# The low-rank gate's rows placed beside the queries' columns in the opening of a two-block transformer kernel

## The reference, cut to what matters

```
h = rms_norm(x, norm_mix_g[l]) * (1.0 + sc_m) + sh_m
proj = jnp.einsum('bsd,de->bse', h, w_in[l])
(a_q, a_k, a_v, b_q, b_ff, b_fb, b_i, b_g,
 c_q, c_k, c_v, c_g, c_lrf, c_lrb, gates) = split_cols(proj, IN_SIZES)

q = to_heads(q_cols, GC_HEADS) * GC_KEY_DIM ** -0.5      # recurrence "c"
k = to_heads(k_cols, GC_HEADS)
def log_decay(lr, w2, bias):
    z = (jnp.einsum('bsr,rk->bsk', lr, w2) + bias).astype(jnp.float32)
    return to_heads(jax.nn.log_sigmoid(z) / GC_GATE_NORMALIZER, GC_HEADS)
la_f = log_decay(lr_fwd, gate_w2[0], gate_b[0])
la_b = log_decay(lr_bwd, gate_w2[1], gate_b[1])
```

## Time and profile before

| what | value |
|---|---|
| time, median of 3 runs | 2344.42 us (2342.73 to 2349.59) |
| the profiled execution | 2339.93 us, its span 2338.0 us |
| PE busy | 2267.4 us, 97% of the span |
| DVE, POOL, ACT busy | 1164.4, 1048.3, 999.9 us |

### The profile page before, as it was taken

The page is one execution under the profiler, slowest core; times in us unless marked ns, Lnnn a source line. Parts: engine busy times, 40 slices in busy tenths (PEclk is TensorE's granted clock), DMA queues, the critical chain, the costliest instruction groups (busy, mean ns, idle before and its releaser), DMA issues. The chain is left out here.

```text
span 2338.0 us, 28977 instructions
## 1 busy us (share of the span) xinstructions
PE 2267.4 (97%) x11624; PEld 1887.4 (81%) x11624; DVE 1164.4 (50%) x1765; ACT 999.9 (43%) x1885; POOL 1048.3 (45%) x794
## 2 busy tenths in 40 slices
PE   7899988999999999999999999999999999999998
PEld 4778766778988888888888888878888888888887
DVE  4787887837432122467574334451443345724253
ACT  4665656545533233555552222363332236422224
POOL 2544333445544454532445454544444443544543
PEclk9899999999999999999999999999999999999999
DMA  7221233356222322311213222322222222222221
GB/s 285 82 73 73 108 126 129 123 177 239 90 91 91 108 91 99 108 55 55 73 56 119 96 90 98 116 91 92 73 94 105 90 75 87 92 105 85 99 98 65
DMA packets 42662, 239.79 MB, mean 103 GB/s; under 512 B 5024, under 2 KB 7072, under 8 KB 17184
## 3 DMA queue, kind: packets, MB, share of 16 engines
q1 hardware_dynamic: 39328, 231.23, 27.7%
q10 hardware_dynamic: 3200, 6.71, 1.0%
HBM read 226.38 MB, written 8.39 MB: 100 GB/s over the span
## 5 line engine op out<-in xcount | busy, mean ns | idle before, releaser
L2602 POOL TENSOR_TENSOR WL<-RAW,WH 128x512 fp32r<-128x512 f32 (+1 forms) x692 | 919.9, 1359 | 1139.2 <-ACT WH L1281 1127.9
L727 PE MATMUL PS<-HHI,WH 128*128 128x512 f32 x1496 | 599.0, 400 | 1.7 <-DVE HLO L1865 1.6
L727 PE MATMUL PS<-HHI,WL 128*128 128x512 f32 x1496 | 584.1, 390 | 0.0
L727 PE MATMUL PS<-HLO,WH 128*128 128x512 f32 x1496 | 584.0, 390 | 0.0
L1281 ACT ACTIVATE WH<-RAW 128x512 fp32r<-128x512 f32 (+1 forms) x692 | 379.8, 612 | 394.6 <-PE PS L727 380.1
L727 PEld LDWEIGHTS PS<-HHI,WH 128*128 128x128 f32 x1496 | 281.6, 188 | 75.9 <-issue 13.8
L727 PEld LDWEIGHTS PS<-HHI,WL 128*128 128x128 f32 x1496 | 281.5, 188 | 60.2
L727 PEld LDWEIGHTS PS<-HLO,WH 128*128 128x128 f32 x1496 | 281.9, 188 | 56.5 <-issue 2.2
L727 PE MATMUL PS<-UF,WH 128*128 128x512 f32 (+1 forms) x832 | 223.9, 357 | 0.0
L1865 DVE TENSOR_TENSOR T<-PS,R 128x512 f32<-128x512 f32 x112 | 76.9, 690 | 212.7 <-PE PS L727 204.8
L727 PEld LDWEIGHTS PS<-UF,WH 128*128 128x128 f32 x832 | 148.3, 189 | 22.7
(11 more groups left out here) (354 smaller groups left out, 3575.5 us busy)
## 6 DMA issues: line engine op xcount, KB each, us to landing
RAW<-in_wts SPq DMA_DIRECT2D x190, 1024.0 KB, 4.8
FW<-in_wts SPq DMA_DIRECT2D x6, 1024.0 KB, 17.5
spill<-T SPq DMA_DIRECT2D x24, 256.0 KB, 3.1
RAW<-in_wts SPq DMA_DIRECT2D x8, 768.0 KB, 4.1
GT<-spill SPq DMA_DIRECT2D x20, 256.0 KB, 4.5
X<-in_xt SPq DMA_DIRECT2D x2, 1024.0 KB, 9.3
out_x<-X SPq DMA_DIRECT2D x8, 256.0 KB, 2.2
X<-in_xt SPq DMA_DIRECT2D x2, 768.0 KB, 8.4
```

What stands on the lines that cost most here:

```text
L727: return e.matmul(o_, l, r, start=start, stop=stop)
L2602: return e.tensor_tensor(o_, a, b, f)
```

## The change

Five things change. The unit `lr` gets a place of its own (in the room of the squares SQP, dead by then), so all later units stand in the other slot than before. PE makes the rows of `lr` among those of `cqk`, chunk by chunk, and not behind them, and the gate's two small products follow in banks 7 and 6, from T0[2]. ACT splits `lr` before column 4 and no longer behind column 5; POOL too. ACT copies `cqk`'s first tile, then splits `cv`, then copies the second tile, and issues the sixteen transfers behind all of it. DVE's copy for the small products goes to T0[2] and waits for column 6 and no longer for the first eight transfers.

```diff
@@ -255,7 +255,7 @@
     def slots(self):
 
         at = self.at
-        self.heads = [at["w1", 0], at["w1", 1], at["fi", 0], at["fi", 1], at["sv", 0], at["sv", 1], at["fi", 22], at["fi", 23]]
+        self.heads = [at["lr", 0], at["w1", 0], at["w1", 1], at["fi", 0], at["fi", 1], at["sv", 0], at["sv", 1], at["fi", 22], at["fi", 23]]
         turns = [i for i in self.dense if i not in self.heads]
         self.slot = {i: n % 2 for n, i in enumerate(turns)}
         self.before_in_slot = {i: turns[n - 2] if n > 1 else None for n, i in enumerate(turns)}
@@ -539,13 +539,14 @@
     LEAN = [2.0 ** (2 * h - 1) for h in range(4)]
 
 
-    spare = [(16, ("w", U["out", 1])), (0, ("w", U["up", 3])), (32, ("w", U["wo", 1])), (0, ("logits2", 15)),
+    spare = [(64, ("sum", "mix")), (16, ("w", U["out", 1])), (0, ("w", U["up", 3])), (32, ("w", U["wo", 1])), (0, ("logits2", 15)),
              (16, ("w", P.unit["f0", "dn", 0, 3])), (48, ("w", P.unit["f0", "dn", 1, 3])), (20, ("mix", 23)), (48, ("w", P.unit["sgu", "dn", 4, 1]))]
     WH = {i: WH2[s] for i, s in P.slot.items()}
     WL = {i: WL2[s] for i, s in P.slot.items()}
     for i, (at_, _) in zip(P.heads, spare):
-        WH[i] = place(f"WHH{i}", q0 + at_ * KB, [2048], F32R)
-        WL[i] = place(f"WLH{i}", q0 + at_ * KB + 8 * KB, [2048], F32R)
+        n = P.size(i)[0] * P.size(i)[1]
+        WH[i] = place(f"WHH{i}", q0 + at_ * KB, [n], F32R)
+        WL[i] = place(f"WLH{i}", q0 + at_ * KB + 8 * KB, [n], F32R)
 
     def w_free(i):
 
@@ -920,6 +921,13 @@
                     if k == 7:
                         full(t, i, m)
 
+        def lr_rows(*ks):
+            i = U["lr", 0]
+            for k in ks:
+                t = rows(BANK[i, 0], i, 0, [k], [H[k]], [("h", "mix", k)], k == 0, k == 7)
+                if k == 7:
+                    full(t, i, 0, 0)
+
         q.wait_ge(*at(("vec",)))
         for p in range(4):
             q.wait_ge(*at(("sqp", "mix", p)))
@@ -939,16 +947,24 @@
         qk_rows(1, 2, 3)
         gains(1)
         share(3)
+        lr_rows(0, 1, 2, 3)
         qk_rows(4)
         turn_row(3)
-        qk_rows(5, 6, 7)
-        tiles(U["lr", 0], H, hk("mix"), 0)
-        q.wait_ge(*at(("lw",)))
-        for p in range(2):
-            free(7)
+        lr_rows(4)
+        qk_rows(5)
+        lr_rows(5, 6)
+        qk_rows(6)
+        lr_rows(7)
+        qk_rows(7)
+
+        def low_rank():
+            q.wait_ge(*at(("lw",)))
             q.wait_ge(*at(("ev", U["lr", 0], 0)))
-            mm(PS[:, 7, :], LWT[0:32, 128 * p:128 * p + 128], T0[0][0:32, :], True, True).then_inc(*up("psum", ("zc", p)))
-            holds(7, ("zc_ev", p))
+            for p in range(2):
+                free(7 - p)
+                mm(PS[:, 7 - p, :], LWT[0:32, 128 * p:128 * p + 128], T0[2][0:32, :], True, True).then_inc(*up("psum", ("zc", p)))
+                holds(7 - p, ("zc_ev", p))
+
         def product(r, lv):
             both, _, heads, _, _, eq, ek, _, _ = scan(r)
             if lv < 7:
@@ -1041,6 +1057,7 @@
             t.then_inc(*up("psum", ("folded", j)))
             holds(FOLDED, ("later_mod", j))
 
+        low_rank()
         for step, *a in P.steps:
             if step == "gemm":
                 i, m, k = a
@@ -1469,22 +1486,24 @@
         e.dma_start(LWT[:, :], mixc[:, NM:NM + LW]).then_inc(*up("lw", ("lw",), by=16))
         e.dma_start(MC[:, :], mixc[:, 0:NM]).then_inc(*up("mixc", ("mixc",), by=16))
         e.dma_start(MF[:, :], masks).then_inc(*up("masks", ("masks",), by=16))
+        split_after(i)
         column(4)
         column(5)
         row_out(3)
-        split_after(i)
         column(6)
         column(7)
         for m in range(2):
             q.wait_ge(*at(("t", i, m)))
             q.wait_ge(*at(("h", "mix", 4 + m)))
             e.activation(T0[m][:, :], PS[:, BANK[i, m], :], ACT.Copy, scale=32.0 ** -0.5 if m == 0 else 1.0).then_inc(*up("a_ev", ("ev", i, m)))
+            if m == 0:
+                split_after(U["lr", 0])
+        for m in range(2):
             q.wait_ge(*at(("ev", i, m)))
             for n in range(8):
                 r, c = 64 * (n // 2 % 2) + 32 * (n % 2), 32 * (n // 2)
                 t = e.dma_start(QKC[r:r + 32, n // 4, m, :], T0[m][c:c + 32, :])
                 t.then_inc(*up(f"dupc{m}", *([("qc", m)] if n == 7 else []), by=16))
-        split_after(U["lr", 0])
         q.wait_ge(*at(("lb", 0)))
         e.activation(LB[:, 0:4], LB[:, 0:4], ACT.Exp).then_inc(*up("a_mix", ("lb", 1)))
         q.wait_ge(*at(("lam", 0)))
@@ -2058,11 +2077,11 @@
         column(7)
         i = U["lr", 0]
         q.wait_ge(*at(("t", i, 0)))
-        q.wait_ge(*at(("qc", 0)))
-        e.tensor_copy(T0[0][0:32, :], PS[0:32, BANK[i, 0], :]).then_inc(*up("d_ev", ("ev", i, 0)))
+        q.wait_ge(*at(("h", "mix", 6)))
+        e.tensor_copy(T0[2][0:32, :], PS[0:32, BANK[i, 0], :]).then_inc(*up("d_ev", ("ev", i, 0)))
         for p in range(2):
             q.wait_ge(*at(("zc", p)))
-            ts(PC[:, p, :], PS[:, 7, :], v("gbias", p), None, ADD).then_inc(*up("d_ev", ("zc_ev", p)))
+            ts(PC[:, p, :], PS[:, 7 - p, :], v("gbias", p), None, ADD).then_inc(*up("d_ev", ("zc_ev", p)))
         q.wait_ge(*at(("masks",)))
         e.tensor_copy(MASK[:, 0:896], MF[:, :]).then_inc(*up("d_mix", ("mask",)))
         q.wait_ge(*at(("vec",)))
@@ -2663,9 +2682,9 @@
         column(3)
         split(U["cqk", 0], 2)
         split(U["cqk", 0], 3)
+        split_after(U["cqk", 0])
         column(5)
-        for tag in ("cqk", "lr"):
-            split_after(U[tag, 0])
+        split_after(U["lr", 0])
 
         def decay(p, n):
             if n == 3:
```

## The result

| | kernel before | kernel after |
|---|---|---|
| time, median | 2346.07 us (2342.26 to 2349.59, 19 runs) | 2349.1 us (2346.03 to 2352.46, 19 runs) |
| ratio after / before | | 1.0014 [1.0008, 1.002] |
| profiled execution | 2339.93 us (span 2338.0) | 2352.46 us (span 2350.4) |

By the ratio the change made the kernel 3.3 us slower (1.9 to 4.7; the medians differ by 3.0), against a forecast of 4.1. That is less than the 7.0 us that the prediction names as its step of measurement, and yet the interval lies above 1.

What follows compares the result with a forecast made beforehand. PE, busy in 97% of the span, was taken as the bound, with the gate chain meeting it at product(0, 0). Gate chain 2.2 plus clock 1.9 made 4.1 us, 2344.42 + 4.1 = 2348.5 us; range 2341.5 to 2353.

Steps and rivals of the forecast that it cites:

- Column 6, 2.75 us later: On PE, twelve matmuls of lr ahead of the last turn of shifts delay shift_out(3) and columns 6 and 7 by 2.75 us.
- `cqk`'s first tile, 4.1 us later: On PE, lr's matmuls ahead of the tile fill it 4.1 us later; ACT copies it at 55.2, not 51.12.
- `cv` starts 7.1 us earlier: ACT splits cv right behind the first copy, so PE may start cv at 57.8 in place of 64.89.
- LB's exponential, 4.1 us later: ACT's same instructions in another order take the same time, so LB is reached at 69.1 in place of 64.96.
- The small chain gives back 2.6: Without POOL beside them, DVE's three small instructions ahead of SC's exponential take 0.5 us and not 3.16.
- The scans held up by 1.2: POOL's first quarter of bz 1 holds up DVE's first gate scan by 1.2 us, bounds 0 and 1.25.
- `product(0, 0)`, 2.2 us later: The gate chain brings this PE product at 89.3 in place of 87.06; bounds 0.9 and 4.8 us.
- PE idle for 8 us, low clock, 1.9 us: PE idles about 8 us before product(0, 0), then starts at half clock and loses 1.9 us, bounds 1.6 and 3.4.
- The sum, 4.1: Gate chain 2.2 plus clock 1.9 us make the kernel 4.1 us later after product(0, 0), with nothing behind giving it back.
- Rival A: Gate chain meets PE at about 80 to 84 us, so cv's 7.1 us stay: 2337.3 at best; chance 10%.
- Rival B: No change: chain about as late as before, clock's loss taken in by later waits; 0 to 1 us, 2345; 22%.
- Rival C: DVE's small chain ahead of SC isn't freed from POOL: 6.7 to 8.2 us slower, 2352; chance 16%.

Runs made afterwards that it cites:

- experiment 5: Kernel after with ACT's old order put back (eight transfers, second tile, eight transfers, then cv's split); PE's new order kept: 2349.18 us, ratio 1.0016.
- experiment 8: Kernel after with two unused POOL subtractions added, released by LB's exponential, to run beside DVE's small chain: 2350.77 us, ratio 1.0022.
- experiment 7: Kernel after with POOL's first quarter of bz 1 held back until DVE has made its two gate scans: 2347.18 us, ratio 1.0011.
- experiment 4: Kernel after with 28 unused matmuls filling PE's wait ahead of product(0, 0): 2343.82 us, ratio 0.9995.
- experiment 2: Kernel after with the sixteen transfers issued by SP, ahead of its load of bz 1, and not by ACT: 2337.14 us, ratio 0.9965.
- experiment 1: Kernel after with ACT's exponential of LB put ahead of the sixteen transfer issues: 2351.84 us, ratio 1.0031.
- 9: Kernel after with transfers issued by SP, eight before and eight behind its load of bz 1: 2339.21 us, ratio 0.9968.
- 10: Kernel after with SP issuing eight transfers before and eight behind bz 1's load, and POOL's first bz 1 quarter waiting for the scans: 2339.41 us, ratio 0.9974.
- experiment 6: Kernel before with only ACT's new order (first tile's copy, cv's split, second copy, then sixteen transfers): 2345.05 us, ratio 0.9997.

## Why the prediction was right, step by step

- *Column 6, 2.75 us later.* 45.70 became 49.38: 2.72 net. Right. The step puts 0.229 us for a matmul where its own division gives 0.227; twelve times 0.227 is the 2.72.
- *`cqk`'s first tile, 4.1 us later.* 51.12 became 56.21: 4.13 net. Right, and it is the whole loss of PE's half (experiment 5: +4.10 at LB, +3.98 at the last matmul of `cv`, +4.0 at the product).
- *`cv` starts 7.1 us earlier.* 64.89 became 58.72: 7.1 net. Right.
- *LB's exponential, 4.1 us later.* It is 3.5. The step said that the same instructions in another order take the same time; in experiment 5 they did. In the change's order the first three issues ran beside the splits of `cv` (from 56.89 on), and the copy of the second tile stands beside them too. That hid some 2.8 us of ACT's work, and the sixteen took 2.1 longer: 0.6 net. The step has no load in it: `cv` now leaves its raw buffer early, SP's load follows at 62.79, and the long issues stand behind that load.
- *The small chain gives back 2.6.* From LB's exponential to SC's it took 4.30 us, and takes 1.68: 2.6. Right in size; experiment 8 shows 1.6 of it, the pair's, to be POOL's doing. The Trainium skill ("SBUF — State Buffer", "Who interferes with whom") says that a VectorE instruction with two inputs in SBUF contends with a GpSimd one that reads it; the 2.12 us against 0.36 agree with it. The prediction let the 2.6 us "come back in full" by that rule; as it tells it, for two inputs in SBUF, it covers the pair and not the third instruction, which has one.
- *`bz` 1's quarter no longer waits, 0.55.* It follows the logarithm at once. Right; the scan decides instead.
- *The scans held up by 1.2.* Measured 0.97 (3.31 against 2.34, and 0.96 in experiment 7).
- *`product(0, 0)`, 2.2 us later.* 1.4 net: 0.6 too much from the issues, 0.2 from the scan. In experiment 4, the same chain with quicker issues, it is 0.6 (47.77 against 47.13).
- *PE idle for 8 us, low clock, 1.9 us.* Idle for 7.32 us, clock 0.50 for 5 us, and 2.37 us lost; the whole came back in experiment 4. In three more profiles it was 3.05, 3.12 and 3.34. All of this lies inside the bounds of 1.6 and 3.4; the 5 us of low clock lie between the 3.7 us and the 6.8 us of the two stretches of the earlier trace rows. By the rule of the Trainium skill ("TensorE: Matmul & The Clock Gate", "HAM oscillation — how this bites in real kernels") the loss was certain; the trace agrees for an idle time of 7.3 us.
- *The sum, 4.1.* 3.76 at `product(0, 1)`, 3.98 at `product(0, 3)`, 3.3 (1.9 to 4.7) in the time. The two misses, +0.8 on the chain and -0.5 on the clock, cancel in part, and that the sum is closer than its parts is luck. It holds beyond this one profile: with their own edits' 0.96 and 1.76 us taken out, experiments 7 and 8 have `product(0, 1)` 3.3 and 3.9 us later than before.

Rival A failed where it was said to decide: the chain met PE at 88.5 net and not at 80 to 84. What it needed was the move of experiment 2, by which the chain comes at 80.8 net (81.74 less 0.92), and there the change does gain. Rival B expected a product near 88 and got it (88.5 net), but for another reason, as the scan was held up (0.97); it failed on the clock, and the trace had caught up with nothing at `product(0, 5)`, 131 us net. Rival C failed at the rows of LB.

Open is why experiment 4 gained 4.5 us over the kernel after, where 3.35 are there at `product(0, 3)`; the interval allows it, and dips further on, whose number differs from profile to profile without a cause that I can name, may be part of it. Open too is what makes single issues long. In after and in experiments 1, 4, 7 and 8 every one of over 0.7 us stands behind SP's load, and in 9 and 10 the eight issues ahead of a load took 5.0 us, the eight behind it 6.9 and 5.6. But experiment 2 has one of 1.61 us without a load, and no kernel here moves the load alone.

## What to carry to other kernels

Idle time of an engine is worth filling only up to the next place where a chain over other engines meets it; look for that place first, and for what on the chain has to issue, copy or split behind the thing that is being delayed. Gathered idle time can cost more than itself: here the clock fell in it and the next work started at half speed, for 2.4 to 3.3 us. Transfer issues are work of the queue that makes them (mostly 0.6 us each here, single ones up to 2.6): on an engine whose chain is critical they belong on a queue that has nothing urgent to do. Here a change that loses 3.3 us with them in the way gains some 4 once they are gone. And what frees a path gains nothing where another one ends last: in experiment 6 the 1.3 us that the small chain had won were lost behind `cv`.

## What the runs showed of the hardware

- An issue of a transfer on ACT's queue ran beside ACT's own instructions where its data was there: at 56.89 beside the splits from 56.70 on. The order in the program isn't the order in time between the two.
- The sixteen issues took 10.4 us in two groups in experiment 5 (5.10 and 5.26), 11.17 on SP, 11.46 in experiment 1, 11.3 in experiment 7 and 12.5 in the kernel after. The median is 0.61 us on ACT in all of them; the difference is in a few long issues (2.12 us the longest in after, 0.61 in before and in experiment 5).
- A DVE instruction of 4 elements beside POOL's took as long as what was left of POOL's instruction (2.12 us for two, 0.36 alone); a scan that starts beside a POOL quarter is held up too (3.31 us for the pair, 2.34 without the quarter in experiment 7).
- The low clock outlasted the idle time by 5 us of full work in after (89.5 to 94.5), and by 6.6 to 7.2 us in experiments 1, 7 and 8. Later dips last some 3 to 7 us, with PE busy through them (4.00 of 4.00), and there were three of them behind 100 us in the profile of before and eight in that of after.
